# Prompt attention in pairs of heads: common score steps, one 256-column value matmul for two heads

## The reference

```python
s_c = jnp.einsum('btgjd,bcgd->btgjc', qg, kc).astype(f32) - slopes[None, None, :, :, None] * c_dist[None, :, None, None, :]
p_c = masked_softmax(s_c, c_mask[None, :, None, None, :])
o_c = jnp.einsum('btgjc,bcgd->btgjd', p_c, vc)
...
p_s = masked_softmax(s_s.reshape(b, tq, N_KV, hg, nk * SEL_BLOCK), (s_dist >= 0).reshape(b, tq, N_KV, 1, nk * SEL_BLOCK))
o_s = jnp.einsum('btgjm,btgmd->btgjd', p_s, v_g.reshape(b, tq, N_KV, nk * SEL_BLOCK, HEAD_DIM))
...
p_w = masked_softmax(s_w, w_mask[None, :, None, None, :])
o_w = jnp.einsum('btgjl,blgd->btgjd', p_w, vw)
o = g[:, :, 0] * o_c + g[:, :, 1] * o_s + g[:, :, 2] * o_w
```

## Time and profile before

| | |
|---|---|
| median of 3 runs | 1679.1 us (1677.68 to 1682.85) |
| the profiled execution, its time | 1680.46 us |
| its span (first to last instruction) | 1678.7 us |
| TensorE busy, whole span | 1624.0 us (97%) |
| VectorE, ScalarE, GpSimd busy | 854.6 (51%), 576.9 (34%), 396.6 us (24%) |
| granted TensorE clock, mean | 0.996 |
| the prompt attention stage | first score at 668.39 us, last value matmuls from 911.14 us |

### The profile page before, as it was taken

One profiled execution on the slowest core, in us unless ns is written; L12 is line 12 of the kernel. 1 busy time (PEld: TensorE's weight loads), 2 busy tenths in 40 slices (PEclk: granted clock), 3 DMA queues, 4 the chain that ended last, 5 costly groups with the idle time before them and its releaser, 6 DMA issues. The chain is left out here.

```text
span 1678.7 us, 45635 instructions
## 1 busy us (share of the span) xinstructions
PE 1624.0 (97%) x20051; PEld 1163.1 (69%) x20051; DVE 854.6 (51%) x1790; ACT 576.9 (34%) x1244; POOL 396.6 (24%) x455
## 2 busy tenths in 40 slices
PE   8999999999999999999999999999999999999997
PEld 6788777777777555676767889766578888445443
DVE  3433456556555354776776664541152465624344
ACT  5221344454533213666663111223312211102444
POOL 0212223333331130556444220223100032000120
PEclk9999999999999999999999999999999999999999
DMA  5112000100101314712001976468611420700001
GB/s 168 38 50 57 3 17 17 29 17 16 29 17 35 89 32 101 231 74 86 18 2 62 309 286 208 144 144 193 156 26 25 142 60 1 277 0 1 26 25 50
DMA packets 111450, 136.81 MB, mean 82 GB/s; under 512 B 42940, under 2 KB 93829, under 8 KB 106046
## 3 DMA queue, kind: packets, MB, share of 16 engines
q1 hardware_dynamic: 102002, 84.61, 17.3%
q0 software_dynamic: 9216, 49.29, 9.4%
q10 hardware_dynamic: 36, 0.01, 0.0%
HBM read 121.28 MB, written 17.15 MB: 82 GB/s over the span
## 5 line engine op out<-in xcount | busy, mean ns | idle before, releaser
L1265 PE MATMUL ps<-xnT,rw_side_w 64*64 64x344 f32 x2304 | 219.3, 459 | 1.6 <-issue 0.9
L1265 PEld LDWEIGHTS ps<-xnT,rw_side_w 64*64 64x64 f32 x2304 | 98.1, 135 | 33.6 <-issue 12.9
L2733 PE MATMUL ps<-xnT,zT 128*128 128x344 f32 x384 | 120.1, 457 | 0.0
L2447 POOL TENSOR_SCALAR probs<-probs,row_sums,gates 128x63 f32<-128x63 f32 (+6 forms) x148 | 95.6, 662 | 94.8 <-DVE row_sums L2403 94.3
L2733 PEld LDWEIGHTS ps<-xnT,zT 128*128 128x128 f32 x384 | 69.5, 190 | 33.1 <-issue 3.4
L2352 ACT ACTIVATE probs<-probs,neg_max 128x63 f32<-128x63 f32 (+6 forms) x148 | 87.5, 595 | 0.0
L2325 PE MATMUL ps<-probsT,kvtok 128*64 128x128 f32 x1056 | 75.3, 280 | 0.0
L2298 PE MATMUL ps<-kT,zT 64*128 64x512 f32 (+3 forms) x384 | 72.0, 485 | 2.5 <-DVE neg_max L2393 1.6
L2368 ACT ACTIVATE probsT<-ps 128x512 f32<-128x512 f32 (+1 forms) x80 | 45.9, 574 | 82.3 <-PE ps L2311 82.3
L3443 POOL TENSOR_TENSOR mT<-mT,gate_n 128x258 f32<-128x258 f32 x28 | 23.7, 854 | 211.7 <-DVE gate_n L3406 211.7
L2311 PE MATMUL ps<-ident,probs 128*128 128x128 f32 (+1 forms) x460 | 68.1, 279 | 4.8 <-DVE probsT L2424 3.2
(11 more groups left out here) (625 smaller groups left out, 3584.5 us busy)
## 6 DMA issues: line engine op xcount, KB each, us to landing
w_z<-in_w_in_dram SPq DMA_DIRECT2D x13, 512.0 KB, 5.0
xnT_kept<-xnT SPq DMA_DIRECT2D x1, 4128.0 KB
x_tok<-in_x_prompt_dram SPq DMA_DIRECT2D x8, 512.0 KB
rw_side_w<-in_w_in_dram SPq DMA_DIRECT2D x16, 256.0 KB, 3.3
zT<-in_w_in_dram SPq DMA_DIRECT2D x8, 512.0 KB
ring_k<-in_w_in_dram SPq DMA_DIRECT2D x8, 512.0 KB, 5.3
w_out<-in_w_out_dram SPq DMA_DIRECT2D x1, 4096.0 KB
h_tok<-in_x_prompt_dram SPq DMA_DIRECT2D x8, 512.0 KB, 8.3
```

The lines of the kernel that those rows point to most:

```text
L1265: last = nc.tensor.matmul(k.ps[half(f), bank, 0:CG], w.side[half(e), g // 3 % 2, c, half(f)], k.xnT[half(e), c, third(g)], start=(phase == ...
L2447: nc.gpsimd.tensor_scalar(every, every, ls[:, at:at + 1], k.gates[:, i, gate:gate + 1], ALU.mult, ALU.mult).then_inc(scaled, 1)
L2733: ins = self.nc.tensor.matmul(self.k.ps[:, self.banks[n % nb], 0:CG], self.w[:, t % 2, c, :], self.k.xnT[:, c, g * CG:(g + 1) * CG], start ...
```

## The change

Units are renumbered so that 2w and 2w+1 are two j of the same tile (w from 0 to 15). Steps, pieces and values are then planned by pairs:

- The short parts of both units are packed into common steps: 80 steps in place of 88. The parts are the same 128.
- A piece is one block of 128 keys of both units, (w, branch, t): 148 pieces in place of 160, always four transposes.
- A value matmul takes both units' columns, 256 in place of 128, and there are 296 in place of 592. The gate works on both units at once.
- A piece's turn waits for all scalings of its branch in the second unit, and so for all six of the first. The pair is due four steps after the second unit's last step. `coefs` waits for all exps up to the unit's last step, counted over both units.
- The tiles come in another order, one for j 0 and 1 and one for j 2 and 3.
- `xnT` becomes a third zone of the ring for units 4 to 25, and the four gathers stand ahead of unit 28's scalings instead of unit 16's, with a wait for the turn of the last piece that lies in `xnT`.

```diff
-AT_ORDER = (0, 4, 7, 1, 6, 2, 5, 3)
+AT_ORDER = ((0, 4, 7, 1, 6, 2, 5, 3), (7, 0, 6, 4, 5, 1, 3, 2))
 AT_SHORT_FIRST = (4, 5, 6)
+AT_SPARE, AT_INPUT = AT_RING + 2 * NP, AT_RING + 2 * NP + KC * TT
+AT_FIRST_INPUT, AT_LAST_INPUT = 4, 26
...
-        for n in range(self.N):
-            i = AT_ORDER[n % NT]
+        for pair in range(self.N // 2):
+            i = self.tile(2 * pair)
             full, rest = [], []
...
+            for n in (2 * pair, 2 * pair + 1):
+                for br, w in ((1, self.width(n, 1)), (2, self.width(n, 2)), (0, NCMP)):
+                    cuts = list(range(0, w, 512))
...
-            self.last_step.append(len(self.steps) - 1)
...
+            self.last_step += [max(s for s, parts in enumerate(self.steps) for q in parts if q[0] == n) for n in (2 * pair, 2 * pair + 1)]
...
+        for w in range(self.N // 2):
             self.first_of.append(len(self.pieces))
-            for a in range(0, len(blocks), 2):
-                self.pieces.append(blocks[a:a + 2])
+            for br in (1, 2, 0):
+                self.pieces += [(w, br, t) for t in range(self.tiles(2 * w, br))]
+                self.last_of[w, br] = len(self.pieces) - 1
...
-        while ready < self.N and self.last_step[ready] + AT_LEAD <= s:
+        while ready < self.N // 2 and self.last_step[2 * ready + 1] + AT_LEAD <= s:
...
-EARLY_CHUNKS = 16
+EARLY_CHUNKS = 28
...
+        exped_at = [sum(2 * part[5] for parts in plan.steps[:plan.last_step[n] + 1] for part in parts) for n in range(plan.N)]
...
             def turn(pc):
-                n = plan.pieces[pc][0][0]
-                pe.wait_ge(scaled, 6 * n + max(2 * (3, 1, 2)[br] for _, br, t in plan.pieces[pc]))
+                w, br, t = plan.pieces[pc]
+                m = NCMP if br == 0 else P
+                pe.wait_ge(scaled, 6 * (2 * w + 1) + 2 * (3, 1, 2)[br])
...
             def values(pc):
...
+                for g in range(2):
+                    at = (1 + 2 * br) * P + g * HD
+                    vals = k.vc[:, half(g)] if br == 0 else k.kvtok[:, plan.first_tile(2 * w, br) + t, at:at + HD]
+                    last = nc.tensor.matmul(k.ps[half(g), 6 + w % 2, 0:2 * P], vals, pt[0:m, pc % NPT, 2 * g * P:2 * (g + 1) * P],
+                                            start=(br == 1 and t == 0), stop=(br == 0))
                 last.then_inc(pvd, 1)
...
+                            dve.wait_ge(pt_ps, plan.freed[n, br, g] + 1)
+                        if first and plan.place[n, br, g] >= AT_SPARE:
+                            dve.wait_ge(xn_out, 16)
...
             def coefs(n):
-                dve.wait_ge(expd, 6 * (n + 1))
+                dve.wait_ge(expd, exped_at[n])
...
                 if n == EARLY_CHUNKS:
                     pool.wait_ge(xn_out, 16)
+                    pool.wait_ge(pt_ps, plan.last_input + 1)
```

More of the change, by code:

```diff
@@ L2167, in __init__ @@
                     self.place[n, br, g] = at
                     self.freed[n, br, g] = max(over) if over else None
[L2169 to L2174 removed]
+                    taken = [q for q in taken if not (q[0] < at + w and at < q[1])] + [(at, at + w, last)]
@@ new lines, in __init__, with room @@
+                    if at >= AT_SPARE:
+                        self.last_input = max(self.last_input, last)
+    def room(self, n, w, held):
+        zones = [(0, AT_RING), (AT_RING, AT_SPARE)]
+        if AT_FIRST_INPUT <= n < AT_LAST_INPUT:
+            zones.append((AT_SPARE, AT_INPUT))
+        found = []
+        for lo, hi in zones:
+            for at in [lo] + [q[1] for q in held if lo <= q[0] < hi]:
+                if at + w <= hi and not any(q[0] < at + w and at < q[1] for q in held):
+                    found.append(at)
+        return found
@@ L2197, in first_tile @@
     def first_tile(n, br):
[L2198 removed]
+        return max(0, PromptPlan.tile(n) - 4) if br == 2 else 0
 def store_tokens(sp, k, x, o):
```

112 lines of the change are left out of this document (52 added, 60 removed).

## The result

The changed kernel takes 1707.54 us (median of 4 runs, 1703.81 to 1708.69), the kernel before 1680.97 us on the same chip (4 runs): a ratio of 1.0139, with a 95% interval of 1.011 to 1.0168. It is 26.6 us slower. The forecast was 1701 us and slower, with a range of 1690 to 1711.

The account below looks back on a forecast made before the run. TensorE was taken to bound the stage. -5.8 + 14.6 + 6.5 + 3 + 0.8 + 3 = +22.1 us on the profiled 1680.5 gave 1702.6, less 1.4 for the median: 1701 us, range 1690 to 1711.

Parts of the forecast that it names:

- What bounds the kernel: Attention stage: TensorE is the bound, 233.74 of 244 us busy; the other engines have a third of their time free.
- The 256-column value matmul: Value matmuls on TensorE: half as many with twice the columns bring nothing, 0 us, bounds -1 and +1.
- Fewer drains: TensorE's list: 195 runs of one tile size instead of 231, 0.16 us each, saving 5.8 us.
- Tile 7: Pair's first turn needs eight scalings behind eight exps; TensorE loses 7.3 us in each tile order, +14.6 us, bounds 10 and 18.
- The start: Stage's first 30 us: more masks and eight scalings before first turns, 11.5 us of waits against 5, +6.5, bounds 3 and 9.
- Turns in a row: Longer runs of turns without a value between wait for copies of turned pieces: +3 us, bounds 0 and 6.
- Gathers and tail: Four gathers about 30 us before the stage's end delay the next scalings little: +0.5 to +1 us with the tail's pieces.
- The sum of the waits: Added waits in the stage: tile 7 14.6, start 6.5, turns in a row 3, gathers and tail 0.8 us.
- 35 to 40 us of idle time: Sign expected in the changed profile: TensorE idle some 35 to 40 us in the stage, where 10.8 were.
- The clock: TensorE falls to half speed behind the two tile-7 gaps: 2 x 1.5 = +3 us, bounds 0 and 2 x 3.3.

Follow-up runs that it names:

- e2: Changed kernel with each value matmul of 256 columns split into two of 128: 1712.35 us, ratio 1.0172 to the kernel before.
- e5: Changed kernel with another tile order, branch 1's coefs and scalings issued separately for tiles 1, 3, 7, at most four turns in a row: 1681.53 us.
- e12: e9 with the four early gathers behind the scalings of 30 (tile, head) pairs instead of 28: 1677.43 us, ratio 0.9954 to the kernel before.
- e1: Changed kernel with branch 1's coefs and scalings of tile 7 issued on their own, ahead of the rest: 1699.01 us, ratio 1.0088 to the kernel before.
- e8: e5 with up to five turns in a row again when the queue is long: 1684.62 us, ratio 1.0041 to the kernel before.
- e4: Kernel before with only the four gathers moved, ahead of unit 28's scalings instead of unit 16's: 1682.95 us, ratio 1.0011.
- e3: Changed kernel with 165 unused identity transposes filling eight long TensorE waits, no wait removed: 1699.21 us, ratio 1.0094 to the kernel before.
- e7: Kernel before with each turn waiting for all six scalings of its unit, not only its own branches': 1700.11 us, ratio 1.0119.
- e6: e5 without the separate early coefs and scalings of branch 1: 1695.16 us, ratio 1.0104 to the kernel before.
- e9: e5 with the coefficients' maximum as a tensor_tensor against a constant tile instead of a tensor_scalar: 1678.27 us, ratio 0.9983 to the kernel before.
- e11: e5 run once more, unchanged: 1680.66 us in its one run.
- e10: Kernel before with the coefficients' maximum as a tensor_tensor against a constant tile instead of a tensor_scalar: 1682.53 us, ratio 1.0003.

## Why the prediction was right

The time, the sign and the mechanism came out as forecast: 1707.5 us in a range of 1690 to 1711, by waits at the named places with the clock falling behind them. That the total came so near is partly luck, since two terms were wrong in opposite directions. The stage's +26.3 us are +19.3 of idle time, +12.4 of half speed and -5.3 of work (26.4 with rounding). The terms, one by one:

- **What bounds the kernel.** Right. Only TensorE's idle time and clock moved; the other engines' busy time is unchanged.
- **The 256-column value matmul, 0 us.** Right within the bounds of 1 us: 0.58 us for four records as for eight, and in e2 the width is worth 0.7 us in the values and 1.3 in all of TensorE's work.
- **Fewer drains, -5.8 us.** Right: TensorE's work at full speed is 228.0 us after against 233.3 before, -5.3 for 36 runs fewer. In e5 and e12, with 38 runs fewer, it is 226.9 us: -6.4. The price is not the same for every run, though. Values (with branch 0's) take 4.3 us less for 19 runs, or 0.23 for a run where 0.16 was taken, turns 1.2 less for 12, and scores the same for 5 fewer. No run changed the number of runs alone, so a share of the values' gain can be the width's.
- **Tile 7, +14.6 us.** Right in mechanism, a little too large. Forecast 1.9 at the score and 5.4 at the turn; measured 1.46 and 4.24 in the first order, 1.40 and 5.13 in the second: 12.2 us, within the bounds. The chain is the forecast one, link by link, and e1 confirms its last link. Step 14's exps ended at 712.11, and the six and two scalings took 6.9 us where the sum had 7.3. From the turns of pieces 12 and 13 (706.35) to the waiting turn it is 13.65 us, and 13.7 were forecast. What was mis-sized is TensorE's own list in between: 8.0 us of work where the sum had 6.4, part of it at half speed from 714.0 on. What TensorE lost there to the clock it did not lose to the wait.
- **The start, +6.5 us.** Half of it. The waits up to 700 us add up to 6.4 us where 3.3 were: +3.1. The walk had 11.5 and 5. How much of it is the packed short parts and how much the eight scalings no run took apart.
- **Turns in a row, +3 us.** Wrong in size: copies end 6.5 us of waits against 5.1, so +1.4. e8 shows that what longer rows cost is mostly the scalings.
- **Gathers and tail, +0.8 us.** e4 gives 0.0 for the gathers in the old plan.
- **The sum of the waits** was forecast as 14.6 + 6.5 + 3 + 0.8 = 24.9 us and is 19.3. The profile was to show 35 to 40 us of idle time and shows 30.1: that sign did not come. Some 4 of the 19.3 lie outside tile 7 and the start: 2.53 us at 754.18, where a turn of tile 6 needs its scalings, and 1 to 1.7 us at three turns near the end.
- **The clock, +3 us.** The term that was mis-sized most. The clock fell in six places of the stage, not in two, and not only behind the long waits: it is also at 0.50 from 756 to 758, behind a wait of 2.53 us. It cost 12.4 us, where 3 were taken and 6.6 was the upper bound; e3 wins back 9.0 of them.

The waits were taken 5.6 us too high, the clock 9.4 too low and the gain from drains 0.5 too large: 4.3 us in all. Another 1.9 come from the start of the sum, since the forecast added to a median of 1679.1 us and the kernel before took 1680.97 beside the changed one. That is all but 0.3 of the 6.5 us between 1701 and 1707.5.

What the runs tell of the kernel: e7, e1 and e2 show that the loss is in readiness, with the half speed behind it (e3), and not in the new matmuls. With the tiles in another order, the branches split and the gathers moved (e12), the same paired plan is 0.5% faster than the kernel before, with a stage of 241.3 us against 245.2. These 3.9 us are 6.4 less work, 0.8 more idle time and 1.7 for one fall of the clock. That the total is faster too rests on one interval, which ends at 0.9986.

## What to carry to other kernels

Before merging two units' work into one instruction, list what must be ready for the merged one and who delivers it, in the order of that engine's list. Here half as many matmuls were worth about 1 us by themselves, since the columns stayed, and the waits and the half speed that came with the pairs cost some 32 us against 5 that they saved. When waits of TensorE are added, look at the granted clock in the windows behind them, and price it apart: here it was 12.4 of a loss of 26.3 us, and filling the waits with useless transposes made the stage 4.7 us shorter. And compare stages by their length within a trace: the time of this stage's start moved by up to 8 us between traces.

## What the runs showed of the hardware

**A VectorE instruction of six columns that takes 5 us.** In e5, e6, e9 and e11 an instruction of 128x6 (0.17 us elsewhere) took 4.78, 5.37, 4.71 and 5.37 us, as a TENSOR_SCALAR and as a TENSOR_TENSOR alike. Each time it began as GpSimd came from four gathers to scalings that had piled up behind them, and GpSimd's scalings ran on undisturbed while it lasted. In the kernel before, the changed one, e1 to e4, e7, e8 and e10 it never took more than 0.84 us, beside GpSimd's scalings too, so their running back to back is not enough; in e12, where VectorE came to it while GpSimd was still issuing gathers, it took 0.17. The Trainium skill's page "SBUF — State Buffer", in the section "SBUF: two separate sides", says that VectorE and GpSimd share a pair of ports under an exclusive lock, that the loser waits for the whole instruction of the other, and that a VectorE instruction in a two-port mode needs the pair, and so does one with two SBUF inputs beside a GpSimd instruction that reads SBUF. By that rule the exchange in e9 would change nothing if the TENSOR_SCALAR ran in such a mode, which no trace here tells; e9 agrees. It speaks of one instruction of GpSimd, though, and in e9 VectorE was held over nine of them (888.97 to 893.5). The gathers' transfers were under way in all four (DMA share 0.91 to 1.00 in e5's rows), and not in e12 when VectorE came to the instruction. But transfers and scalings together are not enough either, as e8 shows some 6 us behind its fourth gather:

```profile
902.62 0.18 DVE L2443 TENSOR_SCALAR row_sums<-row_sums 128x6 f32<-128x6 f32 x1 [4.00 <-ACT kT L2390]
...
903.39 0.21 DVE L2443 TENSOR_SCALAR row_sums<-row_sums 128x6 f32<-128x6 f32 x1 [0.36 <-ACT probs L2390]
```

```profile
903.00:905.00 2.00, 0.45 (x4) 0.48 (x5) 1.01 (x4) 0.84 (x3) 1.87 (x5) 1.00 0.83 340
```

Both began while GpSimd was in a scaling (to 902.77, and from 903.13 on) and took 0.18 and 0.21 us. What is left is the moment at which GpSimd comes from its gathers to the scalings. Why that moment stalls VectorE stays open; no run took the transfers away and left the rest.

**Half speed behind partial idleness.** In e5 the clock also fell at 734.8 us, although TensorE had waited no longer than 1.70 us at a time there. In e11, the same program with a wait of 1.67 us in the same place, it did not; nor did it in e9, and in e12 it did, at 738.3. In e10 it fell at 902.8 us behind a wait of 1.22 us; the kernel before and e4 have the same wait, 1.25 us, and no fall. So waits of this size bring half speed in one execution and not in another, and that is most of the 1.4 to 1.6 us by which a stage's length differs. In the rows after from 712 to 722, it was at full speed in 712 to 714 with 0.54 of 2 us busy and at half in 720 to 722 with all of 2 us busy. So a row's clock does not follow from the same row's busy time, and the rows before it have to be read with it.
